# Tail block of a mixture-of-experts stage in groups of 32 rows, and the residual turned to token rows during routing

## What is computed

```
order = argsort(expert of each assignment)      # tokens x 2 assignments: 1536, then 1024
for each block (slot_tok, e):
    xb = h_pad[tok]
    y  = (silu(xb @ w_gate[e]) * (xb @ w_up[e])) @ w_down[e]     # 1024 -> 512 -> 1024
out[token] += y * weight
h = h + mod[5] * out                             # gated residual
```

## Time and profile before

| | us |
|---|---|
| median of 3 runs | 1990.04 |
| lowest, highest | 1987.12, 1991.53 |
| the profiled execution | 1987.32 |
| its span in the trace | 1985.3 |
| PE busy in the span | 1844.7 (93%) |
| DVE busy | 797.8 (40%) |
| ACT busy | 566.8 (29%) |
| mean granted TensorE clock | 0.972 of 2.4 GHz |

### The profile page before, as it was taken

The page is one execution under the profiler, slowest core; times in us unless marked ns, Lnnn a source line. Parts: engine busy times, 40 slices in busy tenths (PEclk is TensorE's granted clock), DMA queues, the critical chain, the costliest instruction groups (busy, mean ns, idle before and its releaser), DMA issues.

```text
span 1985.3 us, 36978 instructions
## 1 busy us (share of the span) xinstructions
PE 1844.7 (93%) x15991; PEld 1173.5 (59%) x15991; DVE 797.8 (40%) x1710; ACT 566.8 (29%) x1219; POOL 67.3 (3%) x68
## 2 busy tenths in 40 slices
PE   5999999899889989999998999999899897999975
PEld 3554668667654655555554765467667684555533
DVE  3424466678821451011111541356778525111113
ACT  3113233557620321111110523232657422000000
POOL 0000000000010000000000100000000100000001
PEclk9999999989989989999999999999999999999988
DMA  9611110192150777778988512001000306999996
GB/s 379 234 56 43 33 32 22 37 300 68 53 224 22 297 302 290 268 297 302 386 346 342 175 36 98 6 27 54 10 13 1 139 34 251 331 395 396 363 398 223
DMA packets 153025, 361.41 MB, mean 182 GB/s; under 512 B 11704, under 2 KB 73664, under 8 KB 152608
## 3 DMA queue, kind: packets, MB, share of 16 engines
q1 hardware_dynamic: 130128, 316.30, 43.0%
q0 software_dynamic: 6736, 23.99, 3.7%
q10 hardware_dynamic: 16000, 18.75, 2.7%
HBM read 318.26 MB, written 40.77 MB: 181 GB/s over the span
## 4 chain that ended last, share of the span: by engine, by line
PE 81%; DVE 10%; ACT 3%; DMA 3%; issue 2%; SPq 1%; POOL 0%; ACTq 0%; POOLq 0%; DVEq 0%
PE ps L1385 16%; PE ps L974 15%; PE ps L1408 9%; PE ps L1256 7%; PE ps L959 6%; PE ps L1084 4%; PE ps L1118 3%; PE ps L1150 2%; PE ps L919 2%; PE ps L1142 2%; PE ps L1453 2%; PE ps L1366 1%; DMA arena<-in_w_mod 1%; DVE att_small L2172 1%; PE ps L1395 1%
## 5 line engine op out<-in xcount | busy, mean ns | idle before, releaser
L1385 PE MATMUL ps<-arena 128*32 128x256 f32 x6080 | 349.7, 383 | 2.0 <-ACT arena L1869 2.0
L974 PE MATMUL ps<-arena 128*128 128x256 f32 (+2 forms) x1056 | 348.8, 486 | 0.9 <-ACT arena L1650 0.9
L1385 PEld LDWEIGHTS ps<-arena 128*32 128x32 f32 x6080 | 200.4, 111 | 133.3 <-issue 3.7
L974 PEld LDWEIGHTS ps<-arena 128*128 128x128 f32 x1056 | 198.8, 191 | 130.4 <-issue 116.2
L2581 DVE TENSOR_TENSOR arena<-ps,arena 128x128 f32<-128x128 f32 x95 | 27.7, 292 | 413.7 <-ACT arena L1876 413.7
L1408 PE MATMUL ps<-arena 128*32 128x256 f32 x3040 | 183.1, 382 | 0.0
L1256 PE MATMUL ps<-arena 128*128 128x256 f32 (+1 forms) x512 | 143.4, 434 | 2.0 <-DVE arena L2270 2.0
L1084 PE MATMUL ps<-arena 32*128 32x256 f32 (+5 forms) x528 | 130.1, 510 | 3.1 <-ACT arena L1724 2.3
L1876 ACT ACTIVATE arena<-ps 128x128 f32<-128x128 f32 x95 | 26.4, 278 | 370.3 <-PE ps L1385 370.3
L1775 ACT ACTIVATE arena<-ps,att_small 128x768 f32<-128x768 f32 (+2 forms) x160 | 123.3, 773 | 23.8 <-DVE att_small L2172 22.7
L1408 PEld LDWEIGHTS ps<-arena 128*32 128x32 f32 x3040 | 89.3, 109 | 61.2 <-issue 1.0
(11 more groups left out here) (375 smaller groups left out, 2092.2 us busy)
## 6 DMA issues: line engine op xcount, KB each, us to landing
arena<-in_moe_w_gu SPq DMA_DIRECT2D x32, 4096.0 KB, 19.9
arena<-in_moe_w_down SPq DMA_DIRECT2D x32, 2048.0 KB, 12.4
arena<-in_w_mod SPq DMA_DIRECT2D x24, 2048.0 KB, 18.1
y_rows<-zeros_t SPq DMA_DIRECT2D x2, 9216.0 KB, 52.4
arena<-in_w_in SPq DMA_DIRECT2D x6, 2048.0 KB, 8.1
arena<-in_w_in SPq DMA_DIRECT2D x8, 1024.0 KB, 5.7
y_rows<-arena ACTq DMA_DIRECT2D x76, 96.0 KB, 8.0
arena<-in_w_out SPq DMA_DIRECT2D x4, 1536.0 KB, 8.2
```

The costliest lines, as they stand in the source:

```text
L974: last = pe.matmul(PS[:, 4 + k % 2, 0:ch[2]], aT[:, c, t * P:(t + 1) * P], wbuf[:, j % 2, c, 0:ch[2]], start=(c == 0), stop=(c == DC - 1))
L1385: last = pe.matmul(PS[32 * q:32 * q + 32, 2 + g % 2, 0:2 * P], xT(item_par(L, k))[:, a:a + SUB], gate_up_cols(ring_e(L, r), c, q), start=( ...
```

## The change

A tail trip now takes 96 rows in layer 0 and 64 in layer 1 (`TAIL_ROWS`), as three or two groups of 32 in the same form as an item: two gate/up groups, first transposition, (third gate/up, second transposition,) then downs. The capacity of rank 13 falls from 128 to the same figures. The token copy is one DVE instruction, the activations work on 128 columns, outputs are evacuated by ACT in layer 0 and by DVE in layer 1, and four stores of a quarter each replace the one. The slot arithmetic learns that tail blocks are 96 or 64 rows apart: on DVE one linked operation goes, one linked and one unlinked come.

The residual is transposed to token rows in layer 1's routing and copied over `hT` in place by ACT; the 32 transpositions after the last item go, and the final DVE addition reads SBUF where it read PSUM. The wide `gate_row` goes with its eight products and its copy. In layer 1 the three fills before the gates go, the fill before the slot products falls from 3 to 2, and the one after rises from 3 to 6. PE starts layer 1's experts after the last residual copy.

```
+TAIL_ROWS = [96, 64]
-RANK_CAP = [[192, 160, 160, 128, 128, 128] + [96] * 7 + [P] + [96] * FIXED, [96] * 8 + [64] * 5 + [P] + [96] * FIXED]
+RANK_CAP = [[192, 160, 160, 128, 128, 128] + [96] * 7 + TAIL_ROWS[0:1] + [96] * FIXED, [96] * 8 + [64] * 5 + TAIL_ROWS[1:2] + [96] * FIXED]
...
# PE, route_and_rows
-                if L == LAYERS - 1:
-                    fill_clock(3)
+                def residual_rows(i, t):
                     pe.wait_ge(S("ftok_a"), OT0[L] + T)
                     for c in range(DC):
+                        last = pe.transpose(PS[:, 2 * (i % 2) + c // 4, (c % 4) * P:(c % 4 + 1) * P], residual(t)[:, c], ident)
+                    last.then_inc(S("ftok_ps"), 1)
+
+                if L == LAYERS - 1:
+                    for i, t in enumerate(tl[:2]):
+                        residual_rows(i, t)
+                    pe.wait_ge(S("ftok_a"), OT0[L] + T + 2)
+                    for c in range(DC):
                         g = mod4[:, L, 40 + c, 0:1]
-                        pe.matmul(PS[:, c // 4, (c % 4) * P:(c % 4 + 1) * P], bc(g, (0, P)), ident, start=True, stop=True,
-                                  skip_group_check=True)
...
-                fill_clock(3 if L else 7)
+                if L == LAYERS - 1:
+                    pe.wait_ge(S("gates_ready"), 1)
+                    for i, t in enumerate(tl[2:], 2):
+                        residual_rows(i, t)
+                fill_clock(2 if L else 7)
                 pe.wait_ge(S("oh_ready"), L + 1)
...
-                fill_clock(3 if L else 6)
+                fill_clock(6)
...
# PE, experts
+                def tail_gate_up(s):
+                    for c in range(DC):
+                        for q in range(4):
+                            a = c * P + s * SUB
+                            last = pe.matmul(PS[32 * q:32 * q + 32, 2 + s % 2, 0:2 * P], xT(par)[:, a:a + SUB],
+                                             gate_up_cols(TAIL_E[L], c, q), start=(c == 0), stop=(c == DC - 1))
+                    last.then_inc(S("t_pe"), 1)
...
                 with pe.Fori(0, n_tail) as i:
...
+                    pe.wait_ge(S("t_dve"), tail_at(TAIL_DVE, L, lo, i, 1))
+                    pe.wait_ge(S("t_gu"), 16 * (i + lo) + 16)
+                    tail_gate_up(0)
+                    tail_gate_up(1)
+                    tail_h(0, i)
+                    if G == 3:
+                        tail_gate_up(2)
+                        tail_h(1, i)
+                    pe.wait_ge(S("t_wd"), 16 * (i + lo) + 16)
                     pe.wait_ge(S("y_a"), g0 + gt)
...
+                    tail_down(0, i)
+                    tail_h(G - 1, i)
+                    tail_down(1, i)
+                    if G == 3:
+                        pe.wait_ge(S("t_act"), tail_at(TAIL_ACT, L, lo, i, 4))
+                        tail_down(2, i)
...
# PE, the end of the program
-            for i, t in enumerate(out_tiles(1)):
...
-                for c in range(DC):
-                    last = pe.transpose(PS[:, 2 * i + c // 4, (c % 4) * P:(c % 4 + 1) * P], hT[:, c, t * P:(t + 1) * P], ident)
-                last.then_inc(S("tok_ps"), 1)
...
# ACT
+                def residual_rows(i, t):
+                    act.wait_ge(S("ftok_ps"), OT0[L] + OTN[L] + i + 1 + i // 2)
+                    act.activation(residual(t), PS[:, 2 * (i % 2):2 * (i % 2) + 2, :].rearrange("p b (c n) -> p (b c) n", n=P),
+                                   ACT.Copy).then_inc(S("ftok_a"), 1)
...
+                    for q in range(4):
+                        act.dma_start(yt[bass.ds(i, 1)][:, :, :, q * 256:(q + 1) * 256].rearrange("t s b c -> s (t b) c"),
+                                      ysb(par)[32 * q:32 * q + 32, 0:G * 256].rearrange("s (b c) -> s b c", c=256)
+                                      ).then_inc(S("t_y"), 16)
...
# POOL
                     pool.indirect_dma_start(
-                        out=xg(TAIL_I[L] % 2), out_offset=None, in_=dram["f_rows"],
-                        in_offset=bass.IndirectOffsetOnAxis(ap=slot1[:, 0:1], axis=0)).then_inc(S("t_xg"), 16)
+                        out=xg(TAIL_I[L] % 2)[0:n], out_offset=None, in_=dram["f_rows"],
+                        in_offset=bass.IndirectOffsetOnAxis(ap=slot1[0:n, 0:1], axis=0)).then_inc(S("t_xg"), 16)
```

More of the change, by code:

```diff
@@ L59 @@
 C_ID, C_U, C_L, C_ONE = 0, 128, 256, 384
+NOV_J = 7
 C_COS = 512
@@ L502, in first_sub @@
             return SUBS[L].index((k, 0))
+        TAIL_G = [n // SUB for n in TAIL_ROWS]
+        TAIL_PE = [3 * n + 1 for n in TAIL_G]
+        TAIL_DVE = [2 * TAIL_G[0] + 1, 3 * TAIL_G[1] + 1]
+        TAIL_ACT = [2 * TAIL_G[0], TAIL_G[1]]
         TAIL_E, TAIL_I = [EXP - 1, 12], [NI[0], 12]
@@ L531, in slot_before, with tail_at, tail_mark @@
             return None if r == TAIL_E[L] else r - 1 if r > TAIL_E[L] else r
+        def tail_at(per, L, lo, i, n):
+            return per[L] * i + per[0] * lo + n if L else per[0] * i + n
+        def tail_mark(L, what, n):
+            order = [("gu", 0), ("gu", 1), ("ht", 0)]
+            order += [("gu", 2), ("ht", 1), ("dn", 0), ("ht", 2), ("dn", 1), ("dn", 2)] if TAIL_G[L] == 3 else [("dn", 0), ("ht", 1), ("dn", 1)]
+            return 2 * (L + 1) + 2 + order.index((what, n))
         def next_item(L, g):
@@ L675, in build, with residual @@
         restok = ar(A_F, 4 * D).rearrange("p (b n) -> p b n", b=4)
+        def residual(t):
+            return hT[:, :, t * P:(t + 1) * P]
         gate_sub = ar(M_X + 4 * D + 14 * P, 2 * P)
-        gate_row = rows[:, 0:D]
         def y_pair(i, k):
@@ new lines, in tail_h, with tail_down @@
+                def tail_h(s, i):
+                    pe.wait_ge(S("t_dve"), tail_at(TAIL_DVE, L, lo, i, (2 + 2 * s)))
+                    pe.transpose(PS[:, 4 + 3 * (s % 2), 0:P], hid_g(s), ident).then_inc(S("t_pe"), 1)
+                def tail_down(s, i):
+                    pe.wait_ge(S("t_dve"), tail_at(TAIL_DVE, L, lo, i, (3 + 2 * s)))
+                    for c in range(FC):
+                        for q in range(4):
+                            last = pe.matmul(PS[32 * q:32 * q + 32, 5 + s % 2, 0:2 * P], hidT_g(s)[:, c * SUB:(c + 1) * SUB],
+                                             wd[:, c, q * 2 * P:(q + 1) * 2 * P], start=(c == 0), stop=(c == FC - 1))
+                    last.then_inc(S("t_pe"), 1)
@@ L1456, in experts @@
-                    pe.wait_ge(S("t_dve"), 4 * o + 2)
-                    for c in range(FC):
-                        last = pe.transpose(PS[:, 4, c * P:(c + 1) * P], t_hid[:, c * P:(c + 1) * P], ident)
-                    last.then_inc(S("t_pe"), 1)
-                    pe.wait_ge(S("t_dve"), 4 * o + 3)
-                    pe.wait_ge(S("t_wd"), 16 * o + 16)
-                    pe.wait_ge(S("y_a"), g0 + gt)
-                    for half in range(2):
-                        for c in range(FC):
-                            last = pe.matmul(PS[:, 5 + half, :], t_hidT[:, c * P:(c + 1) * P],
-                                             wd[:, c, half * 512:(half + 1) * 512], start=(c == 0), stop=(c == FC - 1))
-                        last.then_inc(S("t_pe"), 1)
@@ new lines, in experts @@
+                        for s in range(G):
+                            act.wait_ge(S("t_pe"), tail_at(TAIL_PE, L, lo, i, tail_mark(L, "dn", s)))
+                            act.activation(ysb(par)[:, s * 256:(s + 1) * 256], PS[:, 5 + s % 2, 0:256], ACT.Copy).then_inc(S("t_act"), 1)
+                    act.wait_ge(S("t_act"), tail_at(TAIL_ACT, L, lo, i, TAIL_ACT[L]))
+                    act.wait_ge(S("t_dve"), tail_at(TAIL_DVE, L, lo, i, TAIL_DVE[L]))
+                    for q in range(4):
+                        act.dma_start(yt[bass.ds(i, 1)][:, :, :, q * 256:(q + 1) * 256].rearrange("t s b c -> s (t b) c"),
+                                      ysb(par)[32 * q:32 * q + 32, 0:G * 256].rearrange("s (b c) -> s b c", c=256)
+                                      ).then_inc(S("t_y"), 16)
@@ new lines, in experts @@
+                    if L == LAYERS - 1:
+                        dve.wait_ge(S(f"y_out{par}"), 16 + 16 * stores(L, par, TAIL_I[L]))
+                        dve.wait_ge(S("t_y"), 64 * (i + lo) + 1)
+                        for s in range(G):
+                            dve.wait_ge(S("t_pe"), tail_at(TAIL_PE, L, lo, i, tail_mark(L, "dn", s)))
+                            dve.tensor_tensor(ysb(par)[:, s * 256:(s + 1) * 256], PS[:, 5 + s % 2, 0:256], gate_sub, mul
+                                              ).then_inc(S("t_dve"), 1)
```

146 lines of the change are left out of this document (60 added, 86 removed).

## The result

| | before | changed |
|---|---|---|
| median (8 runs each) | 1991.68 | 1977.36 |
| lowest, highest | 1984.34, 1995.48 | 1973.94, 1982.23 |
| the profiled execution | 1987.32 | 1981.44 |
| its span | 1985.3 | 1979.6 |
| PE busy in the span | 1844.7 | 1826.1 (92%) |

The ratio is 0.9939, with a 95% interval of 0.9921 to 0.9957: 0.9939 x 1991.68 is 12.1 us less; the two medians themselves differ by 14.3. The two profiled executions differ by 5.9 only, and most of the experiments are about why.

What follows compares the result with a forecast made beforehand. PE, with 81% of the chain, was taken to bound the kernel, but loads layer 1's tail. Layer 0 -7.4 + 0.2, layer 1 routing +0.4 and tail -5.2 gave -12.0; from 1989.0, 1977.0, range 1969 to 1985.

Steps and rivals of the forecast that it cites:

- The mechanism of layer 0: Layer 0's tail: one DVE token copy and three groups at item cadence start modulation earlier, PE gaining 8.9 us.
- a second trip: Rival, tail loop: assignment counts on the chip differ, an extra trip costs at least 15.5, about 1993; chance 0.03.
- starved instructions in the loop: Rival, tail loop: the longer trip body makes PE stall on instruction fetches, about 2005; chance 0.04.
- So I take 6: Layer 0, before combine: 6 us from the tail's last store issue to the first gather, leaving at 1080.5.
- the bound of -6.3: Layer 0: the smallest expected gain at combine, whose forecast was -7.4 within -8.8 to -6.3.
- the wait before combine: Layer 0: gathers formerly covered by PE become late, so PE waits 1.4 for their data.
- Routing: Layer 1's routing: slot products +2.5, six fills +0.5, first two gate/up groups -2.6; together +0.4, from -0.8 to +3.
- Layer 1's tail: Layer 1: loads in a full queue bind, item 14 starts at 1938.4 in place of 1943.64, -5.2, between -3 and -13.0.
- the 2 us that stood as the pessimistic end: Layer 1's tail: item 13's gate/up 2 us late by extra traffic, giving the -3 end.
- The 1.4 for closing the dip: Layer 1's tail: earlier release closes the 312 GB/s gap around 1924 to 1930, worth 1.4.
- The end at 0: Kernel end: removing the 32 transpositions after the last item is worth 0, since DVE waits there for gathered rows.
- residual work lengthens the routing and the queues swallow the rest: Rival: routing +3 at 1.2 GHz, layer 0 -6.3, layer 1 -3; -6.1, down to -4, 1983 to 1985; chance 0.17.

Runs made afterwards that it cites:

- experiment 7: Changed kernel with the last two modulation loads cut to a quarter of their bytes, the rest of those weights not loaded: 1972.62, ratio 0.9895.
- experiments 4 and 10: 4: changed kernel plus four fill products in the wait before combine, 1977.00, ratio 0.9938. 10: changed kernel unedited, third trace, 1979.27, ratio 0.9931.
- experiment 2: Changed kernel without the residual's move (new tail, old routing and old end): 1981.11, ratio 0.9958.
- experiment 3: Changed kernel with layer 1's tail at 96 rows, its third group of 32 being padding: 1981.22, ratio 0.9961.
- Experiment 12: Kernel before plus three fill products where PE waits for ACT in layer 0's tail: 1993.24 against 1992.28, ratio 1.0.
- experiment 8: Changed kernel with layer 0's tail at 128 rows, as four groups in the new overlapped form: 1980.43, ratio 0.9928.

## Why the prediction came out as it did

Three traces of each kernel, averaged by stage:

| stage | before, three traces | changed, three traces | difference of means |
|---|---|---|---|
| T to modulation | 28.60, 31.74, 31.63 | 19.72, 19.71, 19.71 | -10.9 |
| T to combine | 40.95, 44.09, 48.16 | 36.63, 36.03, 36.35 | -8.1 |
| T to first sums | 48.10, 51.24, 56.62 | 46.74, 44.88, 44.97 | -6.5 |
| first sums to M | 546.77, 547.53, 545.97 | 547.63, 546.93, 546.01 | +0.1 |
| M to layer 1's tail | 243.08, 248.17, 243.07 | 242.91, 243.20, 240.48 | -2.6 |
| tail to first addition | 78.31, 80.07, 78.05 | 75.62, 76.01, 75.85 | -3.0 |
| T to end | 931.61, 943.07, 939.77 | 928.92, 927.29, 923.16 | -11.7 |

The predicted 1977.0 met 1977.36, and -12.0 meets -12.1. The changed kernel's other two sets of runs have 1980.69 and 1979.27, 8.6 and 13.7 below the kernel before by their ratios. That is a right total over terms of which two were too large, in part by luck, and it needs saying which part was earned.

- **The mechanism of layer 0 was right, PE's gain exact**: -8.9 forecast, -8.88 measured, the token copy 0.96 for "about 1.0", the three groups at the item cadence. There is one trip a layer, and every wait of PE inside the loop has its releaser, so the rivals of a second trip and of starved instructions in the loop fell.
- **The step that failed is "So I take 6"**, the time from the last store's issue to the first gather. It was 8.8 (8.6 and 8.9 in the other two traces), since the stores, issued earlier, now land no sooner than the modulation's loads, which the earlier trace rows had shown to run on; 2.8 is what it takes with these cut to a quarter (experiment 7). The prediction's 2.2 for a store was one for a store alone. Combine moved by 4.3, not 7.4, outside the bound of -6.3 and below the 5 that the prediction itself had named as a sign of being wrong; against the mean of three traces it moved by 8.1, since the kernel before was slower in the other two. The quantity to use was the end of the loads plus a quiet landing, not an item's median landing.
- **A term was missing**: the wait before combine was forecast as 1.4 and priced at its length. It was 3.85 (3.82 and 4.01 in the other traces), and cost 1.4 to 2.9 more by the clock (experiments 4 and 10). By this pair of traces layer 0 kept 1.4 of the 7.4.
- **Routing was right in its parts**: slot products +2.5 forecast and +2.50 measured, the first two groups -2.75 for -2.6. DVE's tables are ready 2.7 before the slot products start, inside the 1 to 4 named. The +0.5 for six fills did not come: the transpositions start 5.07 after the slot products' end, before 5.08. That the parts nearly cancel agrees with experiment 2.
- **Layer 1's tail: right mechanism, mis-sized.** Loads bind (experiment 3). Item 13's gate/up was held to land as before, at 28.9; it took 32.0, the 2 us that stood as the pessimistic end and one more. But the wait that ends last is item 14's, for its own gate/up. The prediction had this land 46.4 after the tail's first product (1938.0); it landed 49.2 after it. The 1.4 for closing the dip did not come, since the dip comes with the gathers and moved with them. And 1940.2 was the time at which the queues fell quiet, not that of the landing, which in the changed kernel came some 2.5 behind it; the landing before is not in the trace. The queues did fall quiet 1.3 earlier, which is what the bytes left out are worth: 128 x 4 KB are 0.52 MB, where the prediction had 0.4. The first addition gained 2.7, which three traces confirm (-3.0), against -5.2, just outside the bound of -3.
- **PE's own part of that tail was too short as well**: item 12 was to start 13.5 after the tail's first product and started 15.3 after it, with waits of 0.38, 0.38 and 1.03 for DVE between two groups that have no third to cover them. Loads hid this. The bounds of the sum take -8 for the good end of this tail, where its own paragraph has -13.0.
- **The end at 0** stands: 15.35, 16.06 and 16.06 before, 16.02, 16.27 and 15.85 changed.
- **What made up for it lies, by the traces, in the kernel before.** The trace that the sum was read from is the best draw of three (a draw is here a place where TensorE or DVE is slow in one execution and not in the next): it kept the clock in layer 0's tail and in the routing, and had no DVE stall. In the other two the tail's gate/up is 2.8 and 3.0 longer, once the stall adds 3.8 and a slow combine 1.3, once the routing adds about 5. In the new form the tail's gate/up waits only 1.05 for a DVE copy and took 7.11 in all three traces, and only one modulation copy is left on DVE when the gathers start, where the kernel before has four. The prediction had said that its execution lay at the low edge, and used 1989.0 instead; this shift of 1.7 was too small for what it covered, and the over-large terms filled the rest.

How much each draw is worth on average is not settled. Experiment 12 takes one away and finds no gain, with an interval that leaves room for 2.8 at most. Three traces of each kernel are few; that the difference of their means (-11.7) falls on the measured one (-12.1) agrees with this reading and doesn't prove it. So the part of the gain that is given above to the kernel before is argued from six traces, not shown by a run. The cause of the DVE stall wasn't tried: it stands in two of four traces of the old order and in none of ten of the new, where gathers and modulation overlap less.

The rival "residual work lengthens the routing and the queues swallow the rest" named what the first pair of traces shows: layer 0 past its late end, layer 1 at -3, the residual tiles at 1.2 GHz. Its +3 in routing did not come, for M to the tail is -0.2. Its -6.1 on the 1987.32 of that trace would be 1981.2, with 1981.44 measured, though 3.0 of that is the earlier T. The runs, not that pair, decide, and at 8.6 to 13.7 below the kernel before they lie near the forecast.

## What to carry to other kernels

Before a sum is made against one trace, look for its draws: each wait of some 3 us on TensorE may or may not be followed by slow products, and a trace that shows all of them fast gives a kernel before that is better than its median. When a shorter stage issues its stores earlier, they do not land earlier while large loads keep the DMA engines full: take the end of the loads, add a quiet landing, and price the wait that this makes at its length plus the slow products behind it. Where the next stage waits for loads, work taken off TensorE earns little (an extra 5.6 us of it cost 0.5 by the medians, 3.9 in the one trace), unless a later load is waiting for it. Before a dip in GB/s is counted as a gap that can be closed, look at the DMA share beside it: at a share of 1 it is traffic of another kind, and moves with what causes it. The end of a load's traffic is not its landing.

## What was unexpected of the hardware

- The clock after a wait is not the same from one execution to the next: with 2.96 of idle before them 32 rows took 13.97, with 3.08 and 3.17 they took 16.99 and 16.79. Over 12 runs of the kernel before the time went from 1981.53, with a mean granted clock of 0.976, to 1998.85.
- DVE stood still for 5.3 past the end of the product it copies, twice in four traces, at the same instruction, and went on 1.1 after POOL had issued the last of eight gathers, both times. The trace names nothing on this core that it waited for, and the same gathers ran beside the same copies in the other two traces, and beside three of them in experiment 8, without a stall.
- The cadence of 5.58 a group, with transpositions between the column-group products, held in layer 0's tail as in the items (16.9 for three groups), with no gap that the records show; with two groups, in layer 1, two gaps of 0.38 stand in it.
- Stretches in which the DMA engines are at full share and yet move 299 to 351 GB/s, not 406, follow some 4 us behind two gathers of token rows, in both kernels.
